# Expert weights loaded as 16 KB runs of adjacent rows, biases as two fp32r parts picked by one product per half

## The chip, the cores and the metric

The kernel runs on one core of one Trainium2 chip. The metric is device time in microseconds, from a median of runs. All data starts and ends in HBM.

## The reference, cut to what matters

One decoder layer on 256 tokens of 1024 channels, all in float32: attention and a gated recurrence side by side, then a mixture of experts with 32 experts, 4 per token. The change is in the second part:

```python
h2 = rmsnorm(x, norm2_w)
logits = h2 @ router_w + router_b                 # (256, 32)
top_v, top_e = lax.top_k(logits, 4); top_w = softmax(top_v)
# for each expert e, over the tokens xb that chose it:
gu   = xb @ w_gate_up[e] + b_gate_up[e]           # 1024 -> 2048, gate and up in alternating columns
gate = min(gu[:, 0::2], 7); up = clip(gu[:, 1::2], -7, 7)
y    = ((up + 1) * gate * sigmoid(1.702 * gate)) @ w_down[e] + b_down[e]   # 1024 -> 1024
x    = x + sum over the four experts of top_w * y; out = rmsnorm(x, final_norm_w)
```

The weights of all 32 experts are 403 MB (8 MB of w_gate_up and 4 MB of w_down each) and are read once.

## The kernel before, in words

**Order of work.** Up to about 244 us the kernel does projections, attention, recurrence, merge, output projection and router. Then come the 32 experts in order. Each expert has room for 64 tokens (CAP); further rounds follow only if one expert has more, which doesn't happen in the profiled execution. Two experts are a pair: their tokens are gathered together (128 columns, `gather`), and their two outputs are added back together (`combine`). `four(q)` on PE does two pairs; the first and the last `four` are written out, with arguments "biases" and "final".

**Loads.** SP issues nearly all loads (`load(e, m)`). An expert is six loads of 2048 KB: four of w_gate_up (256 rows each) and two of w_down (512 rows each). There are 8 slots in `S`, and one more load is kept elsewhere (`keep`, four loads of 512 KB) so that nine are there or on their way when PE begins with expert 0. From then on SP waits (`used`) until PE has finished with a slot, and issues the next load. In a slot, partition p holds rows k*128+p of the weight: two rows for w_gate_up, so two runs of 8 KB lie one megabyte apart in HBM; four rows for w_down, so four runs of 4 KB. The last w_down load is issued in two halves (L450).

**An expert on PE** (`gate_up`, `down`). hTe holds the gathered tokens, transposed: channel k*128+p in partition p of block k. Per block k there are four products of 128x64 by 128x512 in float32, each two records in the profile: two halves of the columns (banks gu[0], gu[1]), and in each the two column ranges g, which go to partitions 0 to 63 and 64 to 127 of the bank. The bias is added by four more such products with 32 rows (L1492): a one-hot matrix picks row e of b_gate_up. Then DVE and ACT do gate, up and sigmoid (`activate`), the result is transposed in four products and copied (L1504, L1102), and `down` multiplies with w_down (L1513). `keep_clock` are products on constants whose result nobody uses.

**DVE in the loop** (`pair`): activate the first expert, form the gather and scatter matrices, copy its transposed activation, activate the second expert, then `bias_selector` (two copies of 32x64, L1075), `drain_gathered` (the next pair's tokens from two banks, times norm2_w), and the second transposed copy.

**Around the biases.** ACT issues three loads (b_gate_up, b_down, final_norm_w, L659) when the merge is done, just ahead of the statistics of the second norm: squares of two column halves for two token halves (L666), each after DVE's `residual`. DVE's order there is mix_lo (L1003), residual(0,1), normalise(0), residual(1,1) and so on. PE waits for all three loads only before expert 0.

**Float32 as two fp32r parts.** In the first part of the kernel a float32 weight is split: ACT rounds it to fp32r (hi), DVE or POOL subtracts that from the original (lo), and products with both are added up. The change uses the same for the biases.

Of the kernel before, what the change touches and what calls it, by code (L numbers as in the profile page):

```python
# [4 lines left out]
F32 = mybir.dt.float32  # L30
F32R = mybir.dt.float32r
# [5 lines left out]
P = 128  # L37
# [100 lines left out]
def hybrid_block(nc, A, out):  # L138
    ctx = ExitStack()
    with ctx:  # L140
        def sb(name, shape, dt=F32):
            return ctx.enter_context(nc.sbuf_tensor(name, shape, dt))
# [24 lines left out]

        XN = sb("XN", [P, TT, D])
# [15 lines left out]
        ohtab = CST[0:E, 896:896 + E]  # L184
# [41 lines left out]
        GU_B = mpage(8, 2)[0:E, :]  # L226
        DN_B = mpage(8)[E:2 * E, :]
# [9 lines left out]
        wT = mpage(7)[E:2 * E, 512:768]  # L237
        onehot = mpage(7)[0:E, 768:896].rearrange("p (f s) -> p f s", f=2)
# [9 lines left out]
        n1w, n2w = COLS[:, 0:8], COLS[:, 8:16]  # L248
        lbrow0, lbrow1, hnw = COLS[:, 16:20], COLS[:, 20:24], COLS[:, 24:28]
# [44 lines left out]
        small_loaded, lmask_loaded = sem("small_loaded"), sem("lmask_loaded")  # L294
        w_loaded = [sem(f"w_loaded{s}") for s in range(RING)]
        moe_small_loaded = sem("moe_small_loaded")
# [60 lines left out]
        wgu = A["w_gate_up"].rearrange("l e (k p) n -> (l e) p k n", p=P)  # L357
        wdn = A["w_down"].rearrange("l e (k p) n -> (l e) p k n", p=P)
# [14 lines left out]
        def _(sp):  # L373
# [3 lines left out]
            def load(e, m, slot=None):  # L377

                e, s, slot = e + m // 6, m % 6, (m - 1) % SLOTS if slot is None else slot
                src = wgu[e, :, 2 * s:2 * s + 2, :] if s < 4 else wdn[e, :, 4 * (s - 4):4 * (s - 4) + 4, :]  # L380
                if len(src.shape) == 4:
                    src = src[0]
                dst = gu_slot[slot] if s < 4 else dn_slot[slot]
                sp.dma_start(dst, src).then_inc(slot_loaded[slot], 16)  # L384

            def keep(k):
                sp.dma_start(kept[k], wgu[1, :, 4 + k // 2, 1024 * (k % 2):1024 * (k % 2) + 1024]).then_inc(kept_loaded, 16)
# [61 lines left out]
            for part, done in ((0, slot_loaded[last_slot]), (1, last_loaded)):  # L449
                sp.dma_start(dn_slot[last_slot][:, 2 * part:2 * part + 2, :],  # L450
                             wdn[E - 1, :, 4 + 2 * part:6 + 2 * part, :]).then_inc(done, 16)
# [42 lines left out]
        def _(se):  # L494
            st = Steps(se, act_step)
            for r0, n, name in ((0, 8, "norm1_w"), (8, 8, "norm2_w"), (16, 8, "hgrn_lb_logits"), (24, 4, "hgrn_norm_w")):
                se.dma_start(ROWS[r0:r0 + n, :], A[name].rearrange("a (r c) -> (a r) c", c=P)).then_inc(small_loaded, 16)

# [122 lines left out]
            for dst, src in ((RW, A["router_w"].rearrange("l (k p) e -> p (l k) e", p=P)),  # L621
                             (RB, A["router_b"].to_broadcast([P, E]))):
                se.dma_start(dst, src).then_inc(router_loaded, 16)
# [113 lines left out]
        def _(ve):  # L737
# [9 lines left out]
            drain("rows", v.tensor_copy(COLS[:, 0:28], bank("rows")[:, 0:28]))  # L747
# [258 lines left out]
            residual(1, 1)  # L1006
            weighted_T("h2T00", 0, 0, n2w, HT)
# [77 lines left out]
            def activate(i, half):  # L1085
                c = slice(256 * half, 256 * half + 256)
                ve.wait_ge(gu_filled, i * 2 + half + 1)
                g2 = gu[half][:].rearrange("p (n f) -> p n f", f=2)

                v.tensor_scalar(gate[:, c], g2[:, :, 0], LIMIT, None, ALU.min).then_inc(gate_ready, 1)  # L1090

                v.tensor_scalar(up[:, c], g2[:, :, 1], LIMIT, -LIMIT, ALU.min, ALU.max).then_inc(gu_drained, 1)  # L1092
                ve.wait_ge(gu_drained, i * 2 + half + 3)
                v.scalar_tensor_tensor(out=up[:, c], in0=up[:, c], scalar=1.0, in1=gate[:, c],  # L1094
                                       op0=ALU.add, op1=ALU.mult).then_inc(up_ready, 1)
                ve.wait_ge(up_ready, i * 2 + half + 1)
                ve.wait_ge(sigm_ready, i * 2 + half + 1)
                v.tensor_tensor(act[:, c], up[:, c], sg[:, c], ALU.mult).then_inc(act_ready, 1)  # L1098
# [69 lines left out]
        def _(pe):  # L1168
# [49 lines left out]
            pe.wait_ge(small_loaded, 64)  # L1218
            end(tr(begin("rows")[:, 0:28], ROWS[0:28, :], ident[0:28, 0:28]))
# [243 lines left out]
            def gate_up(q, i, m, b, opening, final=False):  # L1463
# [11 lines left out]
                for s in range(4):  # L1475
# [3 lines left out]
                    if s < 3:  # L1479
# [73 lines left out]
            pe.wait_ge(moe_small_loaded, 48)  # L1553
# [29 lines left out]
def shape_constants():  # L1583
# [15 lines left out]
    c[0:E, 896:896 + E] = np.eye(E)  # L1599
# [25 lines left out]
```

## Time and profile before

| what | value |
|---|---|
| median of 3 runs | 1208.63 us (1208.59 to 1210.9) |
| span of the profiled execution | 1206.6 us; it has no time of its own beside this |
| PE busy | 1112.1 us, 92% |
| PE weight loads busy | 523.0 us, 43% |
| DVE, ACT, POOL busy | 337.5, 212.9, 60.3 us |
| moved by DMA | 438.63 MB in 87355 packets, mean 364 GB/s |
| mean granted TensorE clock | 0.986 of full speed |

The span goes from the first to the last instruction. A busy PE is not PE at its peak, since matmuls are pipelined. A packet is one contiguous run that one of the 16 DMA engines moves. The page of the profile shows shares over the whole span; the experts begin at about a fifth of it.

### The profile page before, as it was taken

The numbers are of one execution on the slowest core, as the hardware profiler recorded it, in microseconds if no ns is written. First come the engines' busy times: TensorE is split into PE (matmuls) and PEld (weight loads), VectorE is DVE, ScalarE is ACT, GpSimd is POOL, SyncE is SP. The second block draws the span as 40 slices with busy tenths as digits, with TensorE's granted clock in tenths as the row PEclk, the third lists the DMA queues.
The fourth block names the chain that finished last, engine by engine and source line by source line (L and its number), as shares of the span: only waits on it lengthen the run. The fifth ranks groups of instructions, "written<-read, shape, count | busy, mean of one in ns | idle before, by whom it ended". The sixth has DMA issues, their size and how long they took to land.

```text
span 1206.6 us, 14149 instructions
## 1 busy us (share of the span) xinstructions
PE 1112.1 (92%) x5763; PEld 523.0 (43%) x5763; DVE 337.5 (28%) x661; ACT 212.9 (18%) x337; POOL 60.3 (5%) x39
## 2 busy tenths in 40 slices
PE   7969999999999999999999999999999999999895
PEld 6858999643343333333333333333333333333231
DVE  5895658431111111112211111111111111111112
ACT  5634565200111101010101010101010101010002
POOL 0590012000000000000000000000000000000000
PEclk9988999999999999999999999999999999999997
DMA  8532646899999999999999999999999999999991
GB/s 306 175 140 71 230 172 226 334 372 375 391 417 417 417 417 418 418 418 418 418 417 418 418 418 418 418 418 418 418 418 417 418 418 418 417 418 417 418 416 58
DMA packets 87355, 438.63 MB, mean 364 GB/s; under 512 B 4796, under 2 KB 7128, under 8 KB 54776
## 3 DMA queue, kind: packets, MB, share of 16 engines
q1 hardware_dynamic: 85264, 435.99, 89.6%
q10 hardware_dynamic: 2056, 2.13, 0.6%
q8 instruction: 27, 0.44, 0.2%
q14 instruction: 8, 0.07, 0.0%
HBM read 437.06 MB, written 1.05 MB: 363 GB/s over the span
## 4 chain that ended last, share of the span: by engine, by line
PE 46%; SPq 30%; DMA 16%; POOL 3%; DVE 2%; issue 2%; ACT 1%; DVEq 0%; ACTq 0%; POOLq 0%
SPq L384 29%; PE PS L1472 16%; DMA S<-in_w_gate_up_dram 16%; PE PS L1243 8%; PE PS L1513 8%; PE PS L1492 2%; PE PS L1451 2%; PE PS L1443 2%; PE PS L1206 1%; POOL w_lo L366 1%; PE PS L1259 1%; DVE M L1102 1%; POOL S L484 1%; PE PS L1262 1%; POOL S L483 1%
## 5 line engine op out<-in xcount | busy, mean ns | idle before, releaser
L1472 PE MATMUL PS<-S,M 128*64 128x512 f32 x2032 | 458.6, 597 | 33.3 <-DMA S<-in_w_gate_up_dram 33.3
L1472 PEld LDWEIGHTS PS<-S,M 128*64 128x64 f32 x2032 | 139.9, 137 | 343.6 <-issue 262.8
L1513 PE MATMUL PS<-S,M 128*64 128x512 f32 x1024 | 228.3, 599 | 27.5 <-DVE M L1102 27.5
L1090 DVE TENSOR_SCALAR M<-PS 128x256 f32<-128x256 f32 x64 | 27.0, 422 | 718.8 <-PE PS L1472 718.1
L1513 PEld LDWEIGHTS PS<-S,M 128*64 128x64 f32 x1024 | 71.0, 137 | 164.2 <-issue 129.1
L684 ACT ACTIVATE M<-M 128x256 f32<-128x256 f32 x64 | 26.7, 417 | 513.5 <-DVE M L1090 513.5
L689 ACT COPY M<-PS 64x512 f32<-64x512 f32 x32 | 18.5, 578 | 337.8 <-PE PS L1513 337.8
L1492 PE MATMUL PS<-M 32*64 32x512 f32 x256 | 61.8, 600 | 0.0
L1443 PE MATMUL PS<-M,XN 128*128 128x128 f32 x512 | 59.8, 275 | 0.0
L1443 PEld LDWEIGHTS PS<-M,XN 128*128 128x128 f32 x512 | 58.5, 192 | 0.5 <-DVE M L1061 0.2
L1451 PE MATMUL PS<-M 128*128 128x512 f32 x120 | 55.5, 605 | 0.0
L366 DVE TENSOR_TENSOR w_lo<-S,hi_a 128x2048 fp32r<-128x2048 f32 (+1 forms) x20 | 42.2, 2126 | 6.2 <-ACT hi_a L526 6.0
L526 ACT CAST hi_a<-S 128x2048 fp32r<-128x2048 f32 (+1 forms) x24 | 38.4, 1623 | 9.1 <-DMA S<-in_w_out_dram 6.9
L1451 PEld LDWEIGHTS PS<-M 128*128 128x128 f32 x120 | 21.6, 189 | 33.7 <-issue 33.7
L1492 PEld LDWEIGHTS PS<-M 32*64 32x64 f32 x256 | 15.0, 131 | 44.6 <-issue 44.6
L1243 PE MATMUL PS<-hT_hi,w_lo 128*128 128x256 f32 x208 | 29.2, 283 | 0.0
L1081 DVE TENSOR_TENSOR M<-PS,COLS 128x512 f32<-128x512 f32 x32 | 22.1, 691 | 23.0 <-PE PS L1443 23.0
L1102 DVE COPY M<-PS 128x512 f32<-128x512 f32 x32 | 21.9, 686 | 22.0 <-PE PS L1504 22.0
L1098 DVE TENSOR_TENSOR M<-M 128x256 f32<-128x256 f32 x64 | 27.2, 425 | 2.2
L1094 DVE SCALAR_TENSOR_TENSOR M<-M 128x256 f32<-128x256 f32 x64 | 27.2, 425 | 2.2
L1243 PEld LDWEIGHTS PS<-hT_hi,w_lo 128*128 128x128 f32 x208 | 26.8, 192 | 0.0
L1092 DVE TENSOR_SCALAR M<-PS 128x256 f32<-128x256 f32 x64 | 26.5, 413 | 0.0
(238 smaller groups left out, 832.3 us busy)
## 6 DMA issues: line engine op xcount, KB each, us to landing
S<-in_w_gate_up_dram SPq DMA_DIRECT2D x127, 2048.0 KB, 25.7
S<-in_w_down_dram SPq DMA_DIRECT2D x63, 2048.0 KB, 30.7
S<-in_w_in_dram SPq DMA_DIRECT2D x10, 2048.0 KB, 8.0
S<-in_w_out_dram SPq DMA_DIRECT2D x2, 2048.0 KB, 7.9
S<-in_w_in_dram SPq DMA_DIRECT2D x2, 1024.0 KB, 9.0
S<-in_moba_up_dram SPq DMA_DIRECT2D x1, 2048.0 KB, 7.6
S<-in_hgrn_up_dram SPq DMA_DIRECT2D x1, 2048.0 KB, 8.0
S<-in_w_down_dram SPq DMA_DIRECT2D x2, 1024.0 KB, 27.9
```

What stands on the lines that cost most here:

```text
L366: tensor_tensor(raw_part(what, j, lo=True), raw_part(what, j), hi_part(PIECES[n][3]), ALU.subtract).then_inc(lo_ready[PIECES[n][2]], 1)
L384: sp.dma_start(dst, src).then_inc(slot_loaded[slot], 16)
L526: st.did(nc.scalar.copy(hi_part(PIECES[n][3]), raw_part(what, j)), hi_ready)
L1094: v.scalar_tensor_tensor(out=up[:, c], in0=up[:, c], scalar=1.0, in1=gate[:, c], op0=ALU.add, op1=ALU.mult).then_inc(up_ready, 1)
L1098: v.tensor_tensor(act[:, c], up[:, c], sg[:, c], ALU.mult).then_inc(act_ready, 1)
L1102: v.tensor_copy(actT, multi[:].rearrange("p (c s) -> p c s", c=4)).then_inc(actT_ready, 1)
L1243: ins = mm(ps[:, T * a:T * a + T], w[:, k, P * a:P * a + P], x[:, k, :], start=(k == 0 and w is w_h and x is hi), stop=(k == kn - 1 and x ...
L1443: ins = mm(dst[:, P * a:P * a + P], XN[:, tt, P * k:P * k + P], sel[:, tt, :], start=(tt == 0), stop=(tt == TT - 1))
L1451: mm(acc[tt][n][:], selT[:, P * tt:P * tt + P], Y[:, 512 * n:512 * n + 512], start=False, stop=True, skip_group_check=True)
L1472: ins = mm(gu[half][64 * g:64 * g + 64, :], hTe[:, k, tok], w, start=(k == 0), stop=(k == KD - 1))
L1492: mm(gu[half][64 * g:64 * g + 64, :], onehot[:, b, :], GU_B[:, c:c + 512], start=False, stop=False)
L1513: ins = mm(multi[64 * n:64 * n + 64, :], actT[:, k, 64 * kh:64 * kh + 64], dn_slot[slot][:, k, 512 * n:512 * n + 512], start=(kh == 0 and ...
```

## The change

In HBM nothing is different; which row lands where is. A load of w_gate_up takes 256 adjacent rows, as before, but partition p now gets rows 2p and 2p+1, one run of 16 KB. A load of w_down takes 512 adjacent rows, partition p rows 4p to 4p+3, also one run of 16 KB. The channel order of everything that meets these weights follows: the normalised tokens are written with even and odd channels of each 256 parted, norm2_w and router_w are loaded in that order, and the product that ends `activate` writes its columns four apart.

The biases are stored in 128 rows: b_gate_up's two column ranges, 32 experts each, twice. ACT rounds all of it to fp32r, DVE replaces the second 64 rows by the remainder. A one-hot matrix of 128x128 per expert picks both parts and both ranges at once, so that there is one fp32r product per half. b_down is loaded after that in the place of the raw biases.

```diff
-        wgu = A["w_gate_up"].rearrange("l e (k p) n -> (l e) p k n", p=P)
-        wdn = A["w_down"].rearrange("l e (k p) n -> (l e) p k n", p=P)
+        wgu = A["w_gate_up"].rearrange("l e (s p k) n -> (l e) s p (k n)", p=P, k=2)
+        wdn = A["w_down"].rearrange("l e (h p c) n -> (l e) h p (c n)", p=P, c=4)
...
-                src = wgu[e, :, 2 * s:2 * s + 2, :] if s < 4 else wdn[e, :, 4 * (s - 4):4 * (s - 4) + 4, :]
+                src = wgu[e, s] if s < 4 else wdn[e, s - 4]
...
-                dst = gu_slot[slot] if s < 4 else dn_slot[slot]
-                sp.dma_start(dst, src).then_inc(slot_loaded[slot], 16)
+                sp.dma_start(S[:, slot, :], src).then_inc(slot_loaded[slot], 16)
...
-            for r0, n, name in ((0, 8, "norm1_w"), (8, 8, "norm2_w"), (16, 8, "hgrn_lb_logits"), (24, 4, "hgrn_norm_w")):
+            for r0, n, name in ((0, 8, "norm1_w"), (8, 8, "hgrn_lb_logits"), (16, 4, "hgrn_norm_w")):
                 se.dma_start(ROWS[r0:r0 + n, :], A[name].rearrange("a (r c) -> (a r) c", c=P)).then_inc(small_loaded, 16)
+                se.dma_start(n2w.rearrange("p (s k) -> p s k", k=2),
+                             A["norm2_w"].rearrange("l (s p k) -> p (l s) k", p=P, k=2)).then_inc(n2w_loaded, 16)
...
-            for dst, src in ((GU_B, A["b_gate_up"][0]), (DN_B, A["b_down"][0]),
-                             (FW, A["final_norm_w"].unsqueeze(0).to_broadcast([P, D]))):
-                se.dma_start(dst, src).then_inc(moe_small_loaded, 16)
+            b_gu = A["b_gate_up"][0].rearrange("e (g n) -> g e n", g=2)
+            for x in range(4):
+                se.dma_start(bias_raw[E * x:E * x + E, :], b_gu[x % 2]).then_inc(bias_loaded, 16)
+            se.dma_start(FW, A["final_norm_w"].unsqueeze(0).to_broadcast([P, D])).then_inc(moe_small_loaded, 16)
...
+                        if tt == 1:
+                            se.wait_ge(bias_loaded, 64)
+                            st.did(nc.scalar.copy(bias_parts, bias_raw), bias_hi_ready)
...
+            se.wait_ge(bias_ready, 1)
+            se.dma_start(DN_B, A["b_down"][0]).then_inc(moe_small_loaded, 16)
...
-                    st.did(v.tensor_scalar(XN[:, tt, c], X[:, tt, c], rstd[:, tt:tt + 1], None, ALU.mult), xn2_ready)
+                    st.did(v.tensor_scalar(XN[:, tt, c].rearrange("p (s k q) -> p s k q", s=2, k=2),
+                                           X[:, tt, c].rearrange("p (s q k) -> p s k q", s=2, k=2),
+                                           rstd[:, tt:tt + 1], None, ALU.mult), xn2_ready)
...
+            ve.wait_ge(bias_hi_ready, 1)
+            st.did(v.tensor_tensor(bias_parts[2 * E:4 * E], bias_raw[2 * E:4 * E], bias_parts[2 * E:4 * E], ALU.subtract),
+                   bias_ready)
             residual(0, 1)
             normalise(0)
...
-                for f in range(2):
-                    v.tensor_copy(onehot[:, f, :], ohtab[:, bass.ds(e + f, 1)].to_broadcast([E, CAP]))
+                rows = rowtab[:, :, bass.ds(e, 2)].unsqueeze(3).to_broadcast([P, 2, 2, CAP])
+                v.tensor_copy(pick.rearrange("p f g s -> p g f s"), rows)
...
-                v.tensor_tensor(act[:, c], up[:, c], sg[:, c], ALU.mult).then_inc(act_ready, 1)
+                v.tensor_tensor(act.rearrange("p (c q) -> p q c", c=4)[:, 64 * half:64 * half + 64, :],
+                                up[:, c].rearrange("p (q c) -> p q c", c=4), sg[:, c].rearrange("p (q c) -> p q c", c=4),
+                                ALU.mult).then_inc(act_ready, 1)
...
-                                for g in range(2):
-                                    c = 1024 * g + 512 * half
-                                    mm(gu[half][64 * g:64 * g + 64, :], onehot[:, b, :], GU_B[:, c:c + 512],
-                                       start=False, stop=False)
+                                mm(gu[half][:], pick[:, b].rearrange("p g s -> p (g s)"),
+                                   bias_parts[:, 512 * half:512 * half + 512], start=False, stop=False,
+                                   skip_group_check=True)
```

router_w is loaded in the new channel order (pieces of 256 bytes, before 128), and its load stays where it was.

## Rows read from the trace of the kernel before

**Rows 1.** The page: engines; the span in 40 slices, rate.

```profile
PE 1112.1 (92%) x5763; PEld 523.0 (43%) x5763; DVE 337.5 (28%) x661; ACT 212.9 (18%) x337; POOL 60.3 (5%) x39
GB/s 306 175 140 71 230 172 226 334 372 375 391 417 417 417 417 418 418 418 418 418 417 418 418 418 418 418 418 418 418 418 417 418 418 418 417 418 417 418 416 58
```

**Rows 2.** The chain that ended last: start us, us, what. A start of experts.

```profile
247.60 10.45 PE PS L1472 x48
...
361.14 10.30 PE PS L1472 x48
...
416.98 10.30 PE PS L1472 x48
...
566.40 25.35 DMA S<-in_w_gate_up_dram
...
686.87 25.35 DMA S<-in_w_gate_up_dram
...
1135.17 5.35 PE PS L1472 x16
```

**Rows 3.** Stretches: us, PE, PEld, DVE, ACT, POOL busy, PEclk, DMA share, GB/s.

```profile
250.00:300.00 50.00, 48.27 (x226) 18.10 (x224) 10.42 (x27) 3.20 (x7) 0.00 (x0) 0.97 0.94 373
300.00:350.00 50.00, 49.22 (x226) 17.00 (x223) 7.82 (x21) 5.59 (x10) 0.00 (x0) 1.00 0.97 396
```

**Rows 4.** Timeline of the tail: the last loads and the last down product.

```profile
1146.89 9.59 SPq L450 DMA_DIRECT2D S<-in_w_down_dram  x2
1179.03 7.09 PE L1513 MATMUL PS<-S,M 128*64 128x512 f32 x32 [0.78 <-DVE M L1102]
```

**Rows 5.** DMA view of 5 us: from 435 us (w_gate_up), from 475 us (w_down).

```profile
DMA packets 273, 2.11 MB, mean 421 GB/s; under 512 B 16, under 2 KB 16, under 8 KB 16
...
DMA packets 504, 2.04 MB, mean 407 GB/s; under 512 B 16, under 2 KB 16, under 8 KB 495
```

**Rows 6.** The chain again: fp32r products of 128x512, and the bias products.

```profile
225.26 1.81 PE PS L1256 x8
...
371.44 1.86 PE PS L1492 x8
```

**Rows 7.** Timeline of DVE at the end of a pair: start us, us, line.

```profile
405.87 0.43 DVE L1098 TENSOR_TENSOR M<-M 128x256 f32<-128x256 f32 x1
406.21 0.28 DVE L1075 COPY M<-CST 32x64 f32 x2
406.76 0.69 DVE L1081 TENSOR_TENSOR M<-PS,COLS 128x512 f32<-128x512 f32 x1 [0.28 <-PE PS L1443]
408.55 0.69 DVE L1081 TENSOR_TENSOR M<-PS,COLS 128x512 f32<-128x512 f32 x1 [1.09 <-PE PS L1443]
```

**Rows 8.** Timeline around the bias loads, then their time to landing.

```profile
207.79 0.35 ACTq L659 DMA_DIRECT2D M<-in_b_gate_up_dram  x1
208.65 0.48 ACTq L659 DMA_DIRECT2D M<-in_final_norm_w_dram  x1
220.61 2.28 DVE L1003 TENSOR_TENSOR mix_lo<-M,mix_hi 128x2048 fp32r<-128x2048 f32 x1
221.48 0.29 ACT L669 ACTIVATE SMALL<-SMALL 128x1 f32<-128x1 f32 x1
225.29 0.69 DVE L981 TENSOR_TENSOR X<-PS,X 128x512 f32<-128x512 f32 x1 [2.40 <-PE PS L1262]
228.77 0.88 DVE L991 TENSOR_SCALAR XN<-X,SMALL 128x512 f32<-128x512 f32 x2
...
M<-in_final_norm_w_dram ACTq DMA_DIRECT2D x1, 512.0 KB, 12.0
M<-in_b_gate_up_dram ACTq DMA_DIRECT2D x1, 256.0 KB, 7.6
```

**Rows 9.** Groups by line: form, count, busy us, mean ns, idle before.

```profile
L526 ACT CAST hi_a<-S 128x1024 fp32r<-128x1024 f32 x8 | 8.2, 1044 | 2.0 <-PE PS L1243 2.0
L366 DVE TENSOR_TENSOR w_lo<-S,hi_a 128x1024 fp32r<-128x1024 f32 x4 | 4.8, 1208 | 0.0
```

More of the change, by code:

```diff
@@ L165, in hybrid_block @@
             w_lo = [over(f"w_lo{s}", 4) for s in range(RING)]
+        with ExitStack() as later:
+            later.enter_context(nc.sbuf_tensor("skip_m0", [P, 1024 * 9 + 768], F32))
+            pick = later.enter_context(nc.sbuf_tensor("pick", [P, 256], F32R))[:].rearrange("p (f g s) -> p f g s", f=2, g=2)
+            later.enter_context(nc.sbuf_tensor("skip_m8", [P, 1024], F32))
+            bias_parts = later.enter_context(nc.sbuf_tensor("bias_parts", [P, 1024], F32R))[:]
         XN = sb("XN", [P, TT, D])
@@ L225, in hybrid_block @@
         lgT = mpage(6)[0:E, 512:512 + T]
-        GU_B = mpage(8, 2)[0:E, :]
-        DN_B = mpage(8)[E:2 * E, :]
+        bias_raw = mpage(8)
+        DN_B = mpage(8)[0:E, :]
         FW = mpage(11)
@@ L236, in hybrid_block @@
         selw = mpage(7)[:, 256:512].rearrange("p (t s) -> p t s", t=TT)
[L237 to L238 removed]
+        wT = mpage(7)[0:E, 512:768]
         KEPT = sb("KEPT", [P, D])
@@ L246, in h3 @@
             return ap.rearrange("p (h t) -> p h t", h=GH)
-        n1w, n2w = COLS[:, 0:8], COLS[:, 8:16]
-        lbrow0, lbrow1, hnw = COLS[:, 16:20], COLS[:, 20:24], COLS[:, 24:28]
+        n1w = COLS[:, 0:8]
+        lbrow0, lbrow1, hnw = COLS[:, 8:12], COLS[:, 12:16], COLS[:, 16:20]
+        n2w = SMALL[:, 616:624]
         ss, rstd, eps = SMALL[:, 0:2], SMALL[:, 2:4], SMALL[:, 4:5]
@@ L379, in load @@
                 e, s, slot = e + m // 6, m % 6, (m - 1) % SLOTS if slot is None else slot
-                src = wgu[e, :, 2 * s:2 * s + 2, :] if s < 4 else wdn[e, :, 4 * (s - 4):4 * (s - 4) + 4, :]
-                if len(src.shape) == 4:
+                src = wgu[e, s] if s < 4 else wdn[e, s - 4]
+                if len(src.shape) == 3:
                     src = src[0]
-                dst = gu_slot[slot] if s < 4 else dn_slot[slot]
-                sp.dma_start(dst, src).then_inc(slot_loaded[slot], 16)
+                sp.dma_start(S[:, slot, :], src).then_inc(slot_loaded[slot], 16)
             def keep(k):
-                sp.dma_start(kept[k], wgu[1, :, 4 + k // 2, 1024 * (k % 2):1024 * (k % 2) + 1024]).then_inc(kept_loaded, 16)
+                sp.dma_start(kept[k], wgu[1, 2, :, 1024 * k:1024 * k + 1024]).then_inc(kept_loaded, 16)
             for n, what in enumerate(LOADS):
@@ L449, in _ @@
             for part, done in ((0, slot_loaded[last_slot]), (1, last_loaded)):
-                sp.dma_start(dn_slot[last_slot][:, 2 * part:2 * part + 2, :],
-                             wdn[E - 1, :, 4 + 2 * part:6 + 2 * part, :]).then_inc(done, 16)
+                sp.dma_start(S[:, last_slot, 2048 * part:2048 * part + 2048],
+                             wdn[E - 1, 1, :, 2048 * part:2048 * part + 2048]).then_inc(done, 16)
             sp.wait_ge(rounds_ready, 1)
@@ L495, in _ @@
             st = Steps(se, act_step)
-            for r0, n, name in ((0, 8, "norm1_w"), (8, 8, "norm2_w"), (16, 8, "hgrn_lb_logits"), (24, 4, "hgrn_norm_w")):
+            for r0, n, name in ((0, 8, "norm1_w"), (8, 8, "hgrn_lb_logits"), (16, 4, "hgrn_norm_w")):
                 se.dma_start(ROWS[r0:r0 + n, :], A[name].rearrange("a (r c) -> (a r) c", c=P)).then_inc(small_loaded, 16)
+            with nc.allow_non_contiguous_dma(reason="8-byte pieces, once"):
+                se.dma_start(n2w.rearrange("p (s k) -> p s k", k=2),
+                             A["norm2_w"].rearrange("l (s p k) -> p (l s) k", p=P, k=2)).then_inc(n2w_loaded, 16)
             def root(dst, src, scale):
@@ L620, in _ @@
             filled(se, "pT7")
-            for dst, src in ((RW, A["router_w"].rearrange("l (k p) e -> p (l k) e", p=P)),
+            for dst, src in ((RW.rearrange("p (s k) e -> p s (k e)", k=2),
+                              A["router_w"].rearrange("l (s p k) e -> p (l s) (k e)", p=P, k=2)),
                              (RB, A["router_b"].to_broadcast([P, E]))):
@@ L746, in _ @@
             filled(ve, "rows")
-            drain("rows", v.tensor_copy(COLS[:, 0:28], bank("rows")[:, 0:28]))
+            drain("rows", v.tensor_copy(COLS[:, 0:20], bank("rows")[:, 0:20]))
             st.settle()
@@ L1006, in _ @@
             residual(1, 1)
+            ve.wait_ge(n2w_loaded, 16)
             weighted_T("h2T00", 0, 0, n2w, HT)
@@ L1217, in _ @@
             pe.wait_ge(ident_loaded, 16)
-            pe.wait_ge(small_loaded, 64)
-            end(tr(begin("rows")[:, 0:28], ROWS[0:28, :], ident[0:28, 0:28]))
+            pe.wait_ge(small_loaded, 48)
+            end(tr(begin("rows")[:, 0:20], ROWS[0:20, :], ident[0:20, 0:20]))
             for tt in range(TT):
@@ L1552, in _ @@
             wait_drained(pe, "wT")
-            pe.wait_ge(moe_small_loaded, 48)
+            pe.wait_ge(moe_small_loaded, 32)
+            pe.wait_ge(bias_ready, 1)
             pe.wait_ge(rounds_ready, 1)
@@ L1598, in shape_constants @@
         c[:, 832 + 32 * t:864 + 32 * t] = np.sin(ang[P * t:P * t + P])
-    c[0:E, 896:896 + E] = np.eye(E)
+    for x in range(4):
+        c[E * x:E * x + E, 896 + E * (x % 2):896 + E * (x % 2) + E] = np.eye(E)
     c[:, 1024:1152] = 1.0
```

7 lines of the change are left out of this document (4 added, 3 removed).

## The prediction

> **What bounds the kernel now.** I read the page's engine lines first: PE is busy 92% of the span, and in the line of 40 slices the transfers stand at 416 to 418 GB/s from the twelfth slice to the last but one [rows 1]. Both look full, so the busy shares don't decide, and I went to the chain of waits. It has two regimes. From 361.14 to 416.98 us it stays on PE: two experts take 55.84 us, 27.92 us each, with no wait for weights [rows 2]. From 566.40 us on it jumps to a 25 us transfer of w_gate_up once in four experts: 686.87 - 566.40 = 120.47 us, 30.12 us per expert [rows 2]. One expert is 6 loads of 2048 KB, 12.583 MB; over 30.12 us that is 417.7 GB/s, the rate of the slices. So PE could go at 27.92 us, the weights come at 30.12 us, the eight slots of lead are used up by about 550 us, and from then on the transfers alone set the pace. They are already saturated at about 350 us: two stretches of 50 us give 373 and 396 GB/s before that [rows 3], and then the slices have 417 [rows 1]. At the end PE is the bound again: at 1135.17 us it gets the third w_gate_up load of expert 30 and then runs without waiting for weights; the last w_down half is issued after 1146.89 us and its PE line begins at 1179.03 us [rows 2, 4].
>
> The forecast therefore needs three prices: what 16 KB runs do to the rate, what PE saves where PE is the bound, and what the preparation ahead of expert 0 costs.
>
> **The rate.** The two weights are loaded in different runs now: w_gate_up in pieces of 8 KB, w_down in pieces of 4 KB. I asked the DMA view in stretches of 5 us from 400 to 1150 us. Where all is w_gate_up (270 packets) the mean of 70 stretches is 421.5 GB/s; where all is w_down (510 packets), the mean of 23 is 409.9 (one of each in [rows 5]). Check: 8.389 MB / 421.5 + 4.194 MB / 409.9 = 19.90 + 10.23 = 30.13 us, the period measured. Per engine (a sixteenth of the rate) a 4 KB packet takes 159.9 ns and an 8 KB packet 311.0 ns. A straight line through both is 151.1 ns per 4 KB and 8.8 ns per packet. A 16 KB packet is then 613.2 ns: 427.5 GB/s and 29.43 us per expert, 0.69 us less. No row shows a 16 KB run. The upper end is no cost per packet at all, 433.7 GB/s (29.01 us); the lower end is the slowest form in the trace, 410 (30.70 us). I take the line, since two thirds of the bytes only need one more doubling along it. The stage from about 345 us, where the slices reach the full rate, to 1135 us holds 790 / 30.12 = 26.2 experts: 26.2 x 0.69 = -18.1 us (ends -29.1 and +15.2).
>
> Against the rule of a page: the Trainium skill, "DMA: Bandwidth & Descriptors" (Specifications), puts an HBM limit of about 358 GB/s on a core beside a fabric ceiling of 435. The trace contradicts the first (418 held for 750 us) and the line's end of 433.7 lies just under the second; by the first there would be nothing to win.
>
> **PE.** Per expert the bias is 8 PE records, 4 products of 32x64 by 32x512 in float32, 1.86 us in the chain [rows 6]. The change makes two fp32r products of 128x128 by 128x512. Eight fp32r products of that shape take 1.81 us [rows 6], so two take 0.45; with a change of array layout on both sides I take 0.5 (ends 0.45 and, at the float32 pace, 1.86). PE saves 1.36 us per expert: 26.56. In the middle stage this is worth nothing, for PE then waits 2.87 us per expert where it waited 2.20. It counts in two places. First, the ramp: until 350 us the transfers lose (418 - 373) / 418 x 50 = 5.4 and 2.6 us, 8.0 together [rows 3], because PE has not yet released a slot; that idle time shrinks as PE outruns the transfers faster, about as 2.20 / 2.87, to 6.1: -1.9 us. Second, the tail: the biases of experts 30 and 31 lie on PE's path, 2 x 1.36 = -2.7 us. Is the DMA then late? Nine loads follow the one that lands at 1135.17; before, they end 45.2 us later, at 1180.4, and the last half is needed at 1179.03 + 3/4 of 7.09 = 1184.3. After, they take 44.1 us and are needed 49.2 - 2.7 = 46.5 us on. 2.4 us stay.
>
> **DVE in the loop.** The product that writes act now steps by four elements on all three operands (425 ns today, L1098), and the selector is one copy of 128x256 with permuted output in place of two of 32x64 (0.28 us) [rows 7]. Between the last act product and the first gathered half, DVE has 406.76 - 406.49 = 0.27 us to spare, and the second half waits for PE until 408.55, which leaves 1.1 us more. A 128x256 operation is 0.42 us, 0.14 more than the pair: hidden. If steps made it and each act product twice as long, some 1.3 us would come, and nearly all is still covered by the gathering. Without that cover it would be 0.5 us of PE per expert, paid from its 2.87 us of waiting. Price nothing.
>
> **Before expert 0.** Time there counts in full, since the first slot is released only when expert 0 has been begun and the transfers stand still until then.
> - The normalised rows are now read two elements apart. Two one-tensor operations of 128x512 take 0.88 us, 0.44 each; a two-tensor one of that size takes 0.69 [rows 8]. I price the stepped ones at 0.69: two ahead of the first transposes, +0.5 us; those of the second half are covered by PE's filler product. [...]
> - The biases: four loads of 128 KB in place of two, at 207.79 us. Today the first lands 7.6 us on, and the last of three (896 KB) 12.0 us after its issue, at 220.65 [rows 8]. ACT now waits for them behind its statistics, at about 221.5 us, then casts 128x1024 (1.05 us), and DVE subtracts 64x1024 (1.2 us, by operations of the same row length) [rows 9] before it takes the residual at 225.29. They are behind three loads of 2048 KB on SP. The first should land near 215.4; after it at most 6 more packets per engine, each beside a 16 KB one: 6 x (0.16 + 0.61) = 4.6 us, 220.0. In time by 1.5 us. But if what is queued ahead counts in packets, twice the bytes lie ahead, and they land at 226: +4.5. Queued behind ACT's wait are its squares of the second halves, behind DVE's the residual and with it the router. Ends 0 and +4.5, nearer to 0: +1.
> - norm2_w comes in 8-byte pieces at the start, 512 of them, beside x and the identity; router_w in pieces twice as long. 0 to +1 us together; 0. The load of b_down is later (behind the subtraction) but is needed only after expert 0's first products. 0.
>
> **Sum.** -18.1 - 1.9 - 2.7 + 0.5 + 1 = -21.2 us on a span of 1206.6: 1185.4. The profiled execution has no time of its own beside its span; the median of the runs shown is 1208.63, 2.0 us above it, and that stays: 1187.4, taken as 1187.
>
> **Rivals.**
> 1. Runs beyond 8 KB bring nothing: the difference between the forms is w_down's only, and all comes at 421.5. 29.85 us per expert: 26.2 x 0.27 = -7.1; ramp -2.7; tail -2.7; +1.5. 1198. For it: there are only two points on my line, and at the 5 us grain single stretches scatter from 415 to 428. Against: if a cost per packet is what parts the two forms, it halves once more.
> 2. The change doesn't do what it says: the long runs are cut into the old packets, or the rate is set by something that has no regard to them. 417.7 stays; ramp -3.2, tail -2.7, +1.5: 1204. Against it: today's packets are exactly the runs of the source.
> 3. Slower: the reads of neighbouring partitions are 16 KB apart in HBM where they were 8 and 4, and reads that run side by side meet in the same part of it. Place: every load from 250 us on. Price at today's lowest rate, 410: 30.70 us, +15.2, less 3.8 (ramp) and 2.7, plus 1.5: 1219. It decides from about 416 GB/s down, where 0.15 us per expert eat what PE gives. For it: w_down, with the smallest pitch, is the slower form. Against it: w_down's four pieces per partition are 512 KB apart and w_gate_up's two 1 MB, so strides of that kind exist already, and the new load is one contiguous block. The Trainium skill, "DMA: Bandwidth & Descriptors" (Latency and other measured facts), has a table in which [128 x 16 KiB] tiles halve in rate at row pitches from 512 KiB to 8 MiB; no row here shows a pitch of 16 KB.
> 4. The bias wait bites in full (+4.5 for +1): 1191. It shows as ACT idle at the cast and DVE idle ahead of the residual.
>
> Chances: forecast 0.55 (own range 1181 to 1193), rival 1 0.17, rival 2 0.08, rival 3 0.12, rival 4 0.08. About 0.2% (2.4 us) is what a measurement of this kernel tells from no change. Faster: all but rival 3 and half of rival 2, 0.84; within: 0.04; slower 0.12. The range 1181 to 1204 leaves out rival 3, part of rival 2 and the case without packet cost (1177).
>
> **What would show it.** Stretches at 427 GB/s with about 140 packets per 5 us and an expert every 29.4 us; at 421, rival 1; at 418 or less, 2 or 3. The bias products at 0.45 to 0.5 us per expert and PE-bound experts at 26.6 us between 300 and 500 us. DVE's normalisation at 0.69 us. PE's first expert product near 249 us (247.60 now [rows 2]); at 252, rival 4. PE waiting for w_gate_up more often, though PE's own work is less. If the stage comes at 29.4 us and the time is not below 1195, the sum is wrong at the ramp or the tail.

## The result, and the profile after

The changed kernel takes 1181.59 us (median of 4 runs, 1179.34 to 1182.38) against 1209.57 (4 runs, 1208.59 to 1210.9): a ratio of 0.9768, 95% interval 0.9754 to 0.9782. The forecast was 1187, its range 1181 to 1204. The profiled execution has a span of 1180.2 us (before 1206.6) and took 1182.38 itself.

The page of the changed kernel: engines, and the rate in 40 slices.

```profile
PE 1075.2 (91%) x5571; PEld 518.0 (44%) x5571; DVE 345.7 (29%) x646; ACT 213.7 (18%) x338; POOL 62.4 (5%) x39
...
GB/s 280 212 144 72 194 186 215 287 385 401 395 428 427 426 429 428 428 428 430 428 428 428 428 430 428 428 428 429 429 428 429 428 429 428 428 428 429 427 425 117
```

From the twelfth slice on it stands at 428 where [rows 1] have 417 or 418. PE has 192 records fewer (six per expert) and is still busy 91%, so neither its share nor the lower sum says what the time is made of. The chain of waits does (start us, us, what):

```profile
249.77 10.45 PE PS L1476 x48
...
305.21 10.30 PE PS L1476 x48
...
358.65 10.30 PE PS L1476 x48
368.95 0.67 PE PS L1494 x2
...
613.09 35.28 DMA S<-in_w_gate_up_dram
...
701.19 35.27 DMA S<-in_w_gate_up_dram
...
1105.01 33.95 DMA S<-in_w_gate_up_dram
1138.99 3.65 PE PS L1476 x16
...
1155.85 7.11 PE PS L1516 x32
1164.16 3.51 issue
1167.67 3.69 PE PS L1578 x4
```

- PE-bound experts: 358.65 - 305.21 = 53.44 us for two, 26.72 each, where [rows 2] have 27.92. The bias is 0.67 us of it; it was 1.86 [rows 6].
- Transfer-bound experts: from 613.09 to 701.19 the chain jumps to a w_gate_up load twice per three experts: 88.10 / 3 = 29.37 us. It was 30.12 [rows 2].
- The end: the last jump to a load ends at 1138.96, 16.9 us ahead of the last w_down product; before it was 43.9 us ahead of it (1135.17, 1179.03 [rows 2, 4]). PE now waits for weights until expert 31's, as a faster PE must.
- The last lines, from 1164.16, are a stretch in which PE waits for nothing that the profile shows, and the last products. The prediction has no term for it.

The two stretches that answer to [rows 3] (us, PE, PEld, DVE, ACT, POOL busy, PEclk, DMA share, GB/s), of the changed kernel:

```profile
250.00:300.00 50.00, 48.27 (x224) 18.70 (x222) 11.35 (x27) 3.20 (x7) 0.00 (x0) 0.97 0.95 391
300.00:350.00 50.00, 49.22 (x236) 19.06 (x233) 9.56 (x24) 5.64 (x10) 0.00 (x0) 1.00 0.97 408
```

The transfers lose (428 - 391) / 428 x 50 = 4.3 and 2.3 us, 6.7 together before rounding, where they lost 8.0.

**The ledger of the spans** has three parts, each between two rows of the chain. Expert 0 begins 2.2 us later (249.77, before 247.60). From there to the last w_down product it is 906.08 us, before 931.43: -25.4. From there to the end it is 1180.2 - 1155.85 = 24.4 us, before 1206.6 - 1179.03 = 27.6: -3.2. Together -26.4 us; forecast were -21.2.

### The profile page after: what moved, and what is told of

Its sections match the earlier page's. It is cut to its first block, busy times and chain, and to the rows that moved or that the text cites. A ratio compares the mean times of both kernels' runs of the same rounds, so it can differ in the third digit from the quotient of the medians.

```text
span 1180.2 us, 13741 instructions
## 1 busy us (share of the span) xinstructions
PE 1075.2 (91%) x5571; PEld 518.0 (44%) x5571; DVE 345.7 (29%) x646; ACT 213.7 (18%) x338; POOL 62.4 (5%) x39
## 4 chain that ended last, share of the span: by engine, by line
PE 50%; DMA 42%; POOL 3%; DVE 3%; issue 1%; ACT 1%; DVEq 0%; SPq 0%; ACTq 0%; POOLq 0%
DMA S<-in_w_gate_up_dram 40%; PE PS L1476 17%; PE PS L1516 11%; PE PS L1247 7%; PE PS L1447 3%; PE PS L1455 2%; PE PS L1210 1%; DVE M L1106 1%; PE PS L1201 1%; POOL w_lo L352 1%; PE PS L1263 1%; POOL S L469 1%; DMA S<-in_w_in_dram 1%; POOL S L468 1%; PE PS L1266 1%
## 5 line engine op out<-in xcount | busy, mean ns | idle before, releaser
L1100 DVE TENSOR_TENSOR M<-M 128x256 f32<-128x256 f32 x64 | 38.8, 607 | 2.3
L1083 DVE TENSOR_TENSOR M<-PS,SMALL 128x512 f32<-128x512 f32 x32 | 22.1, 692 | 21.4 <-PE PS L1447 21.4
L1247 PEld LDWEIGHTS PS<-hT_hi,w_lo 128*128 128x128 f32 x208 | 26.8, 192 | 0.0
L1263 PE MATMUL PS<-w_lo,hT_hi 128*128 128x512 f32 x64 | 17.6, 422 | 7.6 <-POOL w_lo L352 7.6
L1494 PE MATMUL PS<-bias_parts,pick 128*128 128x512 f32 x64 | 23.5, 448 | 0.0
## 6 DMA issues: line engine op xcount, KB each, us to landing
S<-in_w_gate_up_dram SPq DMA_DIRECT2D x127, 2048.0 KB, 32.6
```

The source lines that it names most:

```text
L1100: v.tensor_tensor(act.rearrange("p (c q) -> p q c", c=4)[:, 64 * half:64 * half + 64, :], up[:, c].rearrange("p (q c) -> p q c", c=4), sg[ ...
L1247: ins = mm(ps[:, T * a:T * a + T], w[:, k, P * a:P * a + P], x[:, k, :], start=(k == 0 and w is w_h and x is hi), stop=(k == kn - 1 and x ...
L1263: mm(ps[:], hi[:, k, rows], w_l[:, k, :], start=False, stop=False)
```

## Experiments

**1. The bias products alone.** The kernel before with the four loads, the split, the selector and the two fp32r products; weights in their old runs.

```diff
-                                for g in range(2):
-                                    c = 1024 * g + 512 * half
-                                    mm(gu[half][64 * g:64 * g + 64, :], onehot[:, b, :], GU_B[:, c:c + 512], ...)
+                                mm(gu[half][:], pick[:, b].rearrange("p g s -> p (g s)"),
+                                   bias_parts[:, 512 * half:512 * half + 512], ...)
```

> The kernel before with the new bias products alone; the weights stay in runs of 8 and 4 KB. Theory A (transfers set the pace of the experts, by bytes and packets): the period in the middle stays 30.12 us per expert. PE-bound experts take 26.7 us. Gains only on the ramp, where 8.0 us of lost transfer time shrink by 27.92 -> 26.72 to about 5.2 (-2.8 us), and at the end, 2 x 1.2 us; the bias wait costs 0.2. About 1204 us, ratio 0.996. Theory B (a large part of the 28 us measured comes from PE): 1200 us or less. In both, the time to the start of expert 0 stays within 1 us if the later start (249.8 against 247.6 us) has nothing to do with the biases.

Measured: 1201.11 us (6 runs, 1199.4 to 1204.39), ratio 0.9947 (0.9929 to 0.9966), -6.4 us by the ratio. Its stretches:

```profile
250.00:300.00 50.00, 48.27 (x232) 18.92 (x230) 10.44 (x26) 3.20 (x7) 0.00 (x0) 1.00 0.98 390
...
600.00:1100.00 500.00, 436.91 (x2038) 163.29 (x2036) 84.20 (x209) 46.28 (x82) 0.00 (x0) 1.00 1.02 418
```

The steady rate stays at 418, so nothing was won in the 500 us between 600 and 1100: the gain is at the ramp, the tail and the end. Expert 0 to the last w_down product is 5.05 us shorter, and what follows it 3.1 us (24.5 where it was 27.6). Theory A had 1204 us; it had no term for those 3.1 us.

**2. The layout alone.** The changed kernel with the old bias loads, selector and four float32 products.

```diff
-                                mm(gu[half][:], pick[:, b].rearrange("p g s -> p (g s)"), ...)
+                                for g in range(2):
+                                    c = 1024 * g + 512 * half
+                                    mm(gu[half][64 * g:64 * g + 64, :], onehot[:, b, :], GU_B[:, c:c + 512], ...)
```

> The changed kernel with the old float32 bias products. Theory A: 427 to 429 GB/s, 29.4 us per expert once the transfers set the pace: 26.2 x 0.75 = -19.7 us. But PE needs 27.92 us, only 1.4 us less than the transfers, so the ramp loses more, not less (8.0 x 2.20 / 1.44 = 12 us, +4): about 1193 us. PE gets its first wait for weights later than 556 us. Theory B (PE gives much): less than half of the 28 us is left, 1196 or more. If both parts simply add up, this and the bias part together give the 28 us; theory A has them give less than 28 alone (-16 and -5), since each shortens the other's loss.

Measured: 1187.96 us (4 runs, 1187.8 to 1189.76), ratio 0.9841 (0.9823 to 0.9859), -19.2 us. The chain of this kernel has its jumps two experts apart:

```profile
785.57 34.02 DMA S<-in_w_gate_up_dram
...
844.29 34.04 DMA S<-in_w_gate_up_dram
...
1158.56 7.11 PE PS L1509 x32
1166.87 3.50 issue
1170.37 2.08 PE PS L1570 x2
1172.45 1.30 issue
1173.76 5.29 PE PS L1570 x6
```

58.72 / 2 = 29.36 us per expert, as in the whole change. Expert 0 to the last w_down product is 20.3 us shorter; with the 5.05 of experiment 1 that is 25.35, and the whole change has 25.35. That it fits to the hundredth is luck. In the profile of experiment 1 the granted clock over the first expert is 1.00; in those of this experiment, of the kernel before and in the first of the changed kernel it is 0.94. In the second profile of the changed kernel (experiment 3) it is 1.00, the first expert takes 26.78 us where it took 28.48, and the stretch from expert 0 to the last w_down product is 26.8 us shorter than before. So the halves add up within 1.4 us, and by the times they give 6.4 + 19.2 = 25.6 us where experiment 3, run beside them, gives 26.2. After the last w_down product it takes 27.4 us, as before.

Theory A had 1193 us, 5 too many. Its ramp was to lose 12 us of transfer time and lost 9.1 (378 and 400 GB/s in the two stretches, against 428); what the rest of the miss is, no run shows. It also had each half take from the other's gain, 28 - 21 = 7 us in all; by the times 0.6 us are seen, which the noise covers.

**3. The changed kernel once more**, beside experiments 1, 2 and 4.

> The changed kernel once more, as the measure for the others of this chip: 1179 to 1183 us. Three things of its first profile are looked at again: the first projection in float32 (9.53 us against 7.17 before), the start of expert 0 (249.8 us) and the last products of the combine (5.4 us against 8.4 before). If they are the clock's doing and not the change's, at least one of them comes out otherwise this time.

Measured: 1180.42 us (4 runs, 1179.03 to 1183.78), ratio 0.9783 (0.9762 to 0.9803). It asks what the first profile of the changed kernel owes to its execution. There a projection of 32 products near the beginning took 9.53 us; in the profile of the kernel before and in this one, at the same work, 7.17. First the timeline of the first execution, then of this one:

```profile
12.63 9.53 PE L1201 MATMUL PS<-M,S 128*128 128x256 f32 x32 [0.78 <-DVE M L758]
```

```profile
12.77 7.17 PE L1201 MATMUL PS<-M,S 128*128 128x256 f32 x32 [0.78 <-DVE M L758]
```

Expert 0 begins at 249.77 us there, at 247.27 here. The same code does both, so the +2.2 us of the ledger belong to the execution and not to the change. Short values came in experiments 1, 2 and 7, long ones in 5, 6 and 8; the granted clock of the stretch is 1.00 in both kinds, and what decides between them stays open. The last combine, too, differs without a change of code: its eight products take 6.23 us here and 5.40 in the first profile.

**4. The rate by length of run, with nothing else on the core.** One execution. Only loads of w_gate_up, and x copied to the output; all the computation is left out. Ten stretches of 25 MB (12 loads of 2048 KB; 6 of 4096 and 3 of 8192 KB in the two longest forms), each a form of its own: adjacent runs of 2, 4, 8, 16, 32 and 64 KB per partition, then 8, 4 and 2 KB in the old order, then 16 KB again.

```diff
+                    src = flat[pos:pos + P * size]
+                        src = src.rearrange("(p k n) -> p k n", p=P, k=k) if adjacent else \
+                            src.rearrange("(k p n) -> p k n", p=P, k=k)
+                    sp.dma_start(dst, src).then_inc(done[b], 16)
```

> Nothing is computed: the weights are loaded in ten stretches of 25 MB, each with runs of another length, four loads of 2 MB under way. Forms 1 to 6 take one contiguous block of HBM in runs of 2, 4, 8, 16, 32 and 64 KB (the short ones are parted only in SBUF); forms 7 to 9 take 8, 4 and 2 KB runs in the order of the kernel before (runs of one partition far apart); form 10 is 16 KB again. Theory A (a cost per packet of 8.8 ns on 151.1 ns per 4 KB): 388, 410, 421, 428, 431, 432 GB/s, and 421, 410, 388 again in the old order. Theory C (what counts is that a load is one contiguous block of HBM, not how it is cut): forms 1 to 6 all at 428, and 7 to 9 at 421 and 410 and less. A mixture would show in forms 2 and 8, and 3 and 7, which differ in place alone.

Measured, the DMA view inside each stretch, in that order (the column of packets tells the run: half as many at each doubling):

```profile
DMA packets 10754, 21.66 MB, mean 387 GB/s; under 512 B 176, under 2 KB 176, under 8 KB 10754
...
DMA packets 5381, 21.32 MB, mean 410 GB/s; under 512 B 175, under 2 KB 175, under 8 KB 5381
...
DMA packets 2743, 21.15 MB, mean 423 GB/s; under 512 B 161, under 2 KB 161, under 8 KB 161
...
DMA packets 1474, 21.46 MB, mean 429 GB/s; under 512 B 164, under 2 KB 164, under 8 KB 164
...
DMA packets 766, 22.48 MB, mean 432 GB/s; under 512 B 80, under 2 KB 80, under 8 KB 80
...
DMA packets 386, 23.20 MB, mean 430 GB/s; under 512 B 32, under 2 KB 32, under 8 KB 32
...
DMA packets 2751, 21.14 MB, mean 423 GB/s; under 512 B 171, under 2 KB 171, under 8 KB 171
...
DMA packets 5370, 21.34 MB, mean 410 GB/s; under 512 B 160, under 2 KB 160, under 8 KB 5370
...
DMA packets 8833, 17.80 MB, mean 387 GB/s; under 512 B 144, under 2 KB 144, under 8 KB 8833
...
DMA packets 1540, 22.35 MB, mean 430 GB/s; under 512 B 176, under 2 KB 176, under 8 KB 176
```

The line of the prediction, 151.1 ns per 4 KB and 8.8 ns per packet, gives 388, 410, 421, 428, 431 and 432 for 2 to 64 KB: within about 2 GB/s everywhere, also at the 2, 16, 32 and 64 KB that it was not drawn through. The old order has the rate of the adjacent one at 2, 4 and 8 KB, though neighbouring partitions start 16 KB apart in HBM in the adjacent forms up to 16 KB and 8, 4 and 2 KB apart in the old order. So it is a price per packet, and where the runs lie relative to one another does not matter in these forms: rivals 1, 2 and 3 all fall here. The Trainium skill, "HBM Reference" (Specifications (TRN2)), puts a core that streams alone at about 425 GB/s, bounded by its DMA engines; 429 at 16 KB and 432 at 32 KB agree within 2%, and 387 at 2 KB shows that the figure needs the run's length beside it.

**5. Long runs for w_down alone, new bias.** w_gate_up goes back to its two 8 KB runs.

```diff
-                src = wgu[e, s] if s < 4 else wdn[e, s - 4]
+                src = wgu[e, :, 2 * s:2 * s + 2, :] if s < 4 else wdn[e, s - 4]
```

> The new bias products, w_down in 16 KB runs, w_gate_up in the old order with runs of 8 KB. If only the packets' length sets the pace (theory A), an expert takes 8.389 MB / 421.5 + 4.194 MB / 428.6 = 19.90 + 9.79 = 29.69 us, and the time lies between bias alone (1201.1) and the whole change (1181) as 0.43 of 0.76 us: 1201.1 - 0.57 x 20 = 1190 us, ratio 0.985. If what counts is that both weights are contiguous blocks, or how often SP has to issue, it need not be so.

Measured: 1190.57 us (4 runs, 1189.9 to 1191.88), ratio 0.9858 (0.9841 to 0.9874). Its chain:

```profile
675.33 35.73 DMA S<-in_w_gate_up_dram
...
764.32 35.72 DMA S<-in_w_gate_up_dram
```

Three experts: 88.99 / 3 = 29.66 us. By the line it is 8.389 / 421.5 + 4.194 / 428 = 29.70.

**6. Long runs for w_gate_up alone, new bias.** w_down goes back to its four 4 KB runs, and the act product to writing its columns in order.

```diff
-                src = wgu[e, s] if s < 4 else wdn[e, s - 4]
+                src = wgu[e, s] if s < 4 else wdn[e, :, 4 * (s - 4):4 * (s - 4) + 4, :]
```

> The counterpart: w_gate_up in 16 KB runs, w_down in the old order with runs of 4 KB. Theory A: 8.389 / 428.6 + 4.194 / 409.9 = 19.57 + 10.23 = 29.80 us per expert, 1201.1 - 0.42 x 20 = 1193 us, ratio 0.987. So half as many bytes (w_down) give a little more than the other two thirds, because their packets were half as long.

Measured: 1193.41 us (4 runs, 1191.54 to 1195.51), ratio 0.9874 (0.9858 to 0.9891); four experts are 119.27 us of its chain, 29.82 each, by the line 29.83:

```profile
681.78 30.03 DMA S<-in_w_gate_up_dram
...
801.05 30.03 DMA S<-in_w_gate_up_dram
```

Against experiment 1, long runs in w_down bring 10.8 us by the ratios (0.46 us x 26.2 = 12.1) and in w_gate_up 8.8 (0.30 x 26.2 = 7.9). The intervals of the two ratios overlap; the periods, 29.66 and 29.82 us, tell the two apart. A third of the bytes brings more than the other two thirds, since it had half the runs' length: both halves of the edit were needed, and together they are the change.

These two runs also settle a rival that the kernel before leaves open: that SP's issuing, and not the packets, sets the rate. There SP spends 28 to 30 us of each 30.1 us expert on its six issues (between 583 and 673 us). In experiments 5 and 6 (between 575 and 664 us) it spends 23 to 26 of 29.7 and 29.8 us and has time to spare, and the rate still follows the line.

**7. Sixty PE instructions that are never executed.** The changed kernel with 60 more products in the branch for a second round, which is not taken with these inputs. It tests whether the last combine's cost hangs on where it stands in PE's program.

```diff
                 with pe.Fori(1, ROUNDS) as r:
                     with pe.If(most > r * CAP):
                         pe.wait_ge(gu_drained, r * (2 * E) + 2)
+                        keep_clock(60, gath)
```

> The changed kernel with 60 more products in PE's branch for a second round, which is never taken; nothing that runs is different, PE's program is as long again as before the change. From the last down product to the end of the combine it took 13.5 us in the kernel before and 13.4 with the layout alone (both with a gap of 1.0 to 1.3 us between the second and the third record), and 10.1, 10.3 and 10.9 in the three with the new bias products. Theory D (the gap comes from where these instructions lie in PE's program, which the bias products made shorter): the gap is back, about 13.4 us, and the time is some 3 us longer than the changed kernel's. Theory E (the gap has to do with what PE did before it): still 10 to 11 us.

Measured: 1182.3 us (2 runs, 1181.9 and 1182.7), ratio 0.9788 (0.9768 to 0.9807). Timeline of PE at the end, this kernel:

```profile
1153.17 7.09 PE L1516 MATMUL PS<-S,M 128*64 128x512 f32 x32 [0.79 <-DVE M L1106]
...
1165.35 2.08 PE L1579 MATMUL PS<-M 128*128 128x512 f32 x2 [4.04 <-issue]
1168.28 4.47 PE L1579 MATMUL PS<-M 128*128 128x512 f32 x6 [0.85 <-issue]
```

The same view of the changed kernel:

```profile
1155.85 7.09 PE L1516 MATMUL PS<-S,M 128*64 128x512 f32 x32 [0.78 <-DVE M L1106]
...
1167.67 5.40 PE L1578 MATMUL PS<-M 128*128 128x512 f32 x8 [3.68 <-issue]
```

With the padding the eight products of the combine are cut in two again, 0.85 us apart, as in the kernel before (1.02) and in experiment 2 (1.30); in the changed kernel, experiment 1 and experiment 3 they run through. From the end of the last w_down product to that of the combine it is 12.5 us, where theory D had about 13.4 and theory E 10 to 11. From the start of that product to the end of the span it takes 26.5 us; the five profiles with the new bias products, no padding and the combine in its old place have 24.4 to 25.7, and none of them has the gap. So code that never runs brings the gap back. The padding moves the combine's place in PE's program and lengthens what is jumped over, and which of the two does it is not told apart. By the time itself the 2 us are not told apart: two runs, and an interval that holds the ratio of experiment 3.

**8. The combine directly behind the last expert.** The changed kernel with its last eight products written twice: once ahead of the branch, under the opposite condition, and once inside it for the case of more rounds.

```diff
+            with pe.If(most < CAP + 1):
+                finish()
             with pe.If(most > CAP):
...
+                finish()
```

> The changed kernel with PE's last combine written twice: at once behind the last expert where no second round is needed, and behind the rounds otherwise. In the profile of the changed kernel PE stands still for 3.5 us after ACT has copied the last output, while it passes over the code of the rounds; then its 8 records begin at the low level of the clock and take 5.4 us (3.6 where the clock is high). If the way past that code costs the 3.5 us, the combine starts 0.2 us after the copy and runs at the high level: 3.5 + 1.8 = 5 us less, 1176 us, ratio 0.974. If the 3.5 us are something else (a branch alone), 0 to 2 us.

Measured: 1175.68 us (4 runs, 1173.53 to 1176.95), ratio 0.973 (0.9714 to 0.9746). Timeline of PE:

```profile
1154.24 7.09 PE L1516 MATMUL PS<-S,M 128*64 128x512 f32 x32 [0.78 <-DVE M L1106]
1161.26 1.12 PE L1399 MATMUL PS<-CST 128*128 128x512 f32 x2
1162.71 3.69 PE L1570 MATMUL PS<-M 128*128 128x512 f32 x8 [0.33 <-ACT M L685]
```

PE waits 0.33 us for ACT where it stood 3.68 us on nothing, and the products take 3.69 us where they took 5.40. The stretch of the combine (columns as above), first in this kernel, then in the changed one:

```profile
1162.70:1166.40 3.70, 3.69 (x8) 1.44 (x8) 1.29 (x2) 2.26 (x5) 0.00 (x0) 1.00 0.02 4
```

```profile
1167.60:1171.20 3.60, 3.53 (x5) 1.51 (x6) 0.00 (x0) 0.00 (x0) 0.00 (x0) 0.53 0.02 5
```

The granted clock is 1.00, the level of 2.4 GHz, where it was 0.53, near that of 1.2: without the idle time the engine keeps its clock. From the last w_down product to the end it is 19.3 us. This kernel beats both: its ratio to the kernel before, 0.9714 to 0.9746, lies below that of the changed one, 0.9754 to 0.9782, and its median 4.7 to 5.9 us below the two of that (4.6 to 6.4 by the ratios). The Trainium skill, "Runtime: NRT & Kernel Launch" (Instruction fetch mechanics), says that a taken branch whose target is not among the instructions at hand stalls the engine until they are fetched. The trace agrees in place and sign: the stall stood where PE jumps over the code of the second round, and went with the jump. The DMA view has a row that fits: over the stall of the changed kernel (1163.2 to 1167.6 us) it shows one packet of 0.02 MB in the queue that it calls instruction, some 2.5 us before PE goes on, and in this kernel none between 1161.4 and 1162.7 us. Which engine that packet is for it doesn't say, so the fetch is likely and not shown.

## Why the prediction was right, and where its sum was off

The mechanism was right: experiments 1 and 2 each show its half at its place, and they add up. The time came 5.4 us below the forecast, 0.6 us inside the lower end of the range, and the same kernel's second median, 1180.42 us, lies just outside it: that the range held was in part luck. The execution that gave the ledger also began 2.2 us late by chance. By its own steps:

- **The rate: the step held, its size was 8% low.** Forecast 29.43 us per expert, measured 29.37; the old period 30.12. The term was -18.1, and 0.75 x 26.2 is -19.7. The line was drawn through means of 5 us stretches (421.5 and 409.9), and 0.06 us per expert is 0.2% of them. Over 26 experts that is 1.6 us: a small error per period is what a long stage multiplies.
- **PE.** Forecast 0.5 us for the bias products, measured 0.67; a PE-bound expert 26.56, measured 26.72. The ramp: 8.0 us lost before, forecast 6.1, measured 6.7 (-1.3 for -1.9). This term rests on the execution: in experiment 3, the same kernel, the two stretches have 390 and 427 GB/s, a loss of 4.6 us, and the first expert takes 26.78 us where it took 28.48. The rule of proportion itself (2.20 / 2.87) is not borne out: it gives 12 us for experiment 2 and 5 for experiment 1, and these lost 9.1 and 3.3. Tail and ramp together: the stage's 25.4 less the 19.7 of the rate leaves -5.7, forecast -4.6 (-7.1 in experiment 3). How it is split over the two, no run shows: experiment 1, which has them alone, has -5.05, and its stretch from 250 us runs at a granted clock of 1.00 where [rows 3] have 0.97.
- **The transfer at the tail** was not late, as forecast: the last half of w_down keeps no product waiting (0.78 us of idle ahead of the last w_down products, released by DVE, as in [rows 4]).
- **DVE in the loop** was rightly priced at nothing, by wrong sizes and one wrong reading. The act product doesn't step by four on all operands: by the code it reads both sources in order and writes each group of four results 128 elements apart, so that columns that were four apart come to lie side by side. The groups by line, and the selector in the timeline:

```profile
L1100 DVE TENSOR_TENSOR M<-M 128x256 f32<-128x256 f32 x64 | 38.8, 607 | 2.3
...
401.43 0.28 DVE L1077 CAST pick<-CST 128x256 fp32r x1
```

  The act product went from 425 to 607 ns, the selector costs 0.28 us where 0.42 was allowed. The gathering covers both, as the bound in the prediction had it: PE-bound experts take 26.72 us in the changed kernel and also in experiment 1, whose act product takes 425 ns.
- **The normalised rows: this step failed.** Two stepped reads were priced at 0.69 us each (+0.5). Timeline of the changed kernel around the biases (DVE and ACT), then the loads' time to landing:

```profile
225.24 1.05 ACT L663 CAST bias_parts<-M 128x1024 fp32r<-128x1024 f32 x1 [1.33 <-DMA M<-in_b_gate_up_dram]
226.32 1.22 DVE L1002 TENSOR_TENSOR bias_parts<-M,bias_parts 64x1024 fp32r<-64x1024 f32 x1 [1.30 <-ACT bias_parts L663]
227.58 0.69 DVE L976 TENSOR_TENSOR X<-PS,X 128x512 f32<-128x512 f32 x1
231.06 0.88 DVE L986 TENSOR_SCALAR XN<-X,SMALL 128x512 f32<-128x512 f32 x2
...
M<-in_b_gate_up_dram ACTq DMA_DIRECT2D x4, 128.0 KB, 10.6
```

  Two take 0.88 us, to the hundredth what they took [rows 8]: a float32 read from SBUF two elements apart costs nothing more with one tensor operand. Two tensors, with the result scattered as the act product scatters it, cost 43% more (607 ns for 425). The Trainium skill, "VectorE: DVE Perf Modes" (What auto-detection actually checks), ties the step to the mode for 16-bit types alone, and asks nothing of it for a single float32 source. By that reading the term is 0, and the trace agrees: 0.88 us before and after.
- **The bias wait: seen, and free.** It was priced at +1 of 0 to 4.5. ACT did wait for the biases, 1.33 us, and DVE 1.30 for the cast. The biases are there at 225.2; less the 2.1 us by which this execution was already late (its last projection starts at 208.17, before at 206.04) that is 223.1, where 220.0 was forecast and 226 by rival 4. So the landing was forecast 3 us too early, and what rival 4 named is there: the slowest of the four loads lands 13.4 to 13.7 us after its issue in the five profiles with these biases and 16 KB runs of w_gate_up queued ahead (ACT waits 0.9 to 1.3 us), and 9.8 and 10.2 us in experiments 1 and 5, where those runs are 8 KB (ACT doesn't wait). But the residual that DVE takes at 227.58 needs a product that ends at 227.38 in this chain (225.26 before, where the next begins [rows 6]): 0.2 us late, and the chain doesn't go through it (it stays on PE's products until 232.84). The slack stood in [rows 8]: DVE idles 2.40 us ahead of that residual, the subtraction takes 1.2 us of it, and the other 1.2 us could take up a late landing. I had counted the wait from ACT's being ready, and not from DVE's need.
- **After the last expert: a term that the prediction lacked.** It gave the stretch behind the last w_down product no change; it fell by 3.2 us in the profiled execution. Experiment 1 has it (24.5 us), experiment 2 has not (27.4), so it comes with the new bias products. Experiment 7 brings 0.85 us of it back, the gap within the combine, by code that is never executed. Most of the rest goes with the granted clock: 0.50 through the whole combine before, and 0.53 over its first 3.6 us after, 5 of the 8 products. The rows stood in the timeline of the kernel before:

```profile
1191.27 2.08 PE L1574 MATMUL PS<-M 128*128 128x512 f32 x2 [4.09 <-issue]
1194.36 5.28 PE L1574 MATMUL PS<-M 128*128 128x512 f32 x6 [1.02 <-issue]
```

  5.1 us in which PE stands with nothing to wait for, on the path. That was the place to ask what sets it; experiment 8 takes 4.7 to 5.9 us from it, about as much as the new bias products bring in all (6.4).

In sum, for the span: rate -19.7 for -18.1, ramp and tail -5.7 for -4.6, preparation 0 for +1.5 (expert 0 begins 0.3 us earlier than before in experiment 3), behind the last expert -3.2 for 0, the slow projection at the start +2.2 for 0.

## What to carry to other kernels

Where transfers bound a kernel, plot time per packet against run length from the forms that the trace already has: two points gave the third within 0.2%, and the shortest runs are the first to lengthen even if they carry the fewer bytes. Work taken off an engine that waits for weights comes back only where it doesn't wait, at the ramp and the tail, and those can be measured alone. Read the chain to its last line: a stall before the last products, with nothing behind it to wait for, may be a jump over code that isn't run, and most of it was had back here by writing the common case ahead of the branch. And profile the same kernel twice before you read a microsecond out of a ledger: here two executions differed by 2.5 us at the start of the experts and by 1.4 us between there and the last w_down product.

## What the runs showed of the hardware

- By the fitted line each DMA packet costs 8.8 ns on its engine besides its bytes (151.1 ns per 4 KB): 387, 410, 423, 429, 432 and 430 GB/s were measured at runs of 2, 4, 8, 16, 32 and 64 KB. 32 KB runs were not tried in the kernel; by the line they are worth an estimated 12.583 / 428 - 12.583 / 431 = 0.2 us per expert.
- With short runs SP is held at the issue itself: between 560 and 640 us it spends 11.7 to 13.3 us on each pair of w_down loads in the kernel before, 5.2 in the changed one. The chain before puts 29% of the span on SP's issues of weights, the chain after puts nothing there and 40% on the transfers. Neither share was time to be had: the transfers ran at their full rate behind both.
- A w_gate_up load now takes 32.6 us from issue to landing (the median), where it took 25.7 in the kernel before, at a higher rate. So the time to landing of a queued transfer doesn't tell its speed; that it is issued earlier and waits longer behind the others is the likely reason.
